# Expert gates of a PEER layer: one-hot matmuls against scattered, adding DMAs into a DRAM table

## What is computed

```python
sub = jnp.einsum("thpc,hpnc->thpn", qh, peer_sub_keys)
v1, i1 = lax.top_k(sub[:, :, 0], PEER_TOPK)
v2, i2 = lax.top_k(sub[:, :, 1], PEER_TOPK)
cand = (v1[..., :, None] + v2[..., None, :]).reshape(T, PEER_HEADS, 256)
vals, cidx = lax.top_k(cand, PEER_TOPK)
e1 = jnp.take_along_axis(i1, cidx // PEER_TOPK, axis=-1)
e2 = jnp.take_along_axis(i2, cidx % PEER_TOPK, axis=-1)
experts = e1 * N_KEYS + e2                      # 128 x 128
gates = jax.nn.softmax(vals, axis=-1)
...
h = jnp.einsum("cd,chkd->chk", xc, jnp.take(peer_u, experts))
a = jax.nn.gelu(h) * gates
y = jnp.einsum("chk,chkd->cd", a, jnp.take(peer_v, experts))
```

## Time and profile before

| | |
|---|---|
| median of 3 runs | 3204.29 us (3204.08 to 3206.46) |
| span of the profiled execution | 3203.0 us, mean granted clock 0.998 |
| its own time | the page gives the span alone; the three runs lie 1.1 to 3.5 us above it |
| busy: TensorE, weight loads, VectorE, ScalarE, GpSimd | 3185.0, 2707.6, 2226.0, 1555.5, 13.7 us |
| weight loads and other DMAs | 610.61 MB, 191 GB/s on the mean |

### The profile page before, as it was taken

The page is one execution under the profiler, slowest core; times in us unless marked ns, Lnnn a source line. Parts: engine busy times, 40 slices in busy tenths (PEclk is TensorE's granted clock), DMA queues, the critical chain, the costliest instruction groups (busy, mean ns, idle before and its releaser), DMA issues.

```text
span 3203.0 us, 42378 instructions
## 1 busy us (share of the span) xinstructions
PE 3185.0 (99%) x17362; PEld 2707.6 (85%) x17362; DVE 2226.0 (69%) x3055; ACT 1555.5 (49%) x1998; POOL 13.7 (0%) x29
## 2 busy tenths in 40 slices
PE   9999999999999999999999999999999999999999
PEld 8888888888888888887888888888888788888887
DVE  6775556677577567766568997766687787865564
ACT  4564444555355455546544555455443344444353
POOL 0000000000000000000000000000000000000000
PEclk9999999999999999999999999999999999999999
DMA  7456665656665666653555666666666665556665
GB/s 252 154 162 218 211 211 180 210 191 191 191 190 190 193 188 192 205 170 111 190 154 171 217 216 189 188 183 224 190 190 212 203 200 173 188 184 192 194 184 171
DMA packets 175825, 610.61 MB, mean 191 GB/s; under 512 B 19201, under 2 KB 27553, under 8 KB 174736
## 3 DMA queue, kind: packets, MB, share of 16 engines
q1 hardware_dynamic: 173648, 599.93, 60.0%
q0 software_dynamic: 1984, 7.99, 0.8%
HBM read 597.36 MB, written 10.49 MB: 190 GB/s over the span
## 4 chain that ended last, share of the span: by engine, by line
PE 97%; DVE 2%; ACT 1%; issue 0%; DMA 0%; SPq 0%; ACTq 0%; DVEq 0%
PE PS L1194 29%; PE PS L1211 16%; PE PS L1213 16%; PE PS L1212 16%; PE PS L1191 15%; PE PS L1414 1%; PE PS L1427 1%; PE PS L1293 1%; DVE LO L1749 0%; PE PS L1247 0%; PE PS L1326 0%; ACT UN L1506 0%; ACT HI L1436 0%; PE PS L1305 0%; PE PS L1223 0%
## 5 line engine op out<-in xcount | busy, mean ns | idle before, releaser
L1749 DVE TENSOR_TENSOR LO<-RAW,HI 128x1024 fp32r<-128x1024 f32 (+1 forms) x1096 | 1325.1, 1218 | 698.0 <-ACT HI L1436 694.7
L1436 ACT ACTIVATE HI<-RAW 128x1024 fp32r<-128x1024 f32 (+1 forms) x1096 | 1148.3, 1054 | 1044.6 <-PE PS L1213 732.5
L1194 PE MATMUL PS<-XX,HI 128*128 128x512 f32 x4032 | 968.4, 391 | 0.0
L1194 PEld LDWEIGHTS PS<-XX,HI 128*128 128x128 f32 x4032 | 739.4, 188 | 145.1 <-issue 2.4
L1211 PE MATMUL PS<-HI,FH 128*128 128x512 f32 x1760 | 692.0, 393 | 1.7 <-DVE LO L1749 1.7
L1213 PE MATMUL PS<-HI,FL 128*128 128x512 f32 x1760 | 685.8, 390 | 0.0
L1212 PE MATMUL PS<-LO,FH 128*128 128x512 f32 x1760 | 684.7, 389 | 0.0
L1191 PEld LDWEIGHTS PS<-XX,LO 128*128 128x128 f32 x4032 | 520.2, 191 | 21.1 <-issue 1.0
L1191 PE MATMUL PS<-XX,LO 128*128 128x256 f32 x4032 | 536.8, 284 | 0.0
L1213 PEld LDWEIGHTS PS<-HI,FL 128*128 128x128 f32 x1760 | 330.3, 188 | 70.1
L1211 PEld LDWEIGHTS PS<-HI,FH 128*128 128x128 f32 x1760 | 330.3, 188 | 69.1 <-DVE LO L1749 2.2
(11 more groups left out here) (286 smaller groups left out, 1667.7 us busy)
## 6 DMA issues: line engine op xcount, KB each, us to landing
RAW<-in_peer_ut SPq DMA_DIRECT2D x256, 512.0 KB, 4.1
RAW<-in_peer_v SPq DMA_DIRECT2D x256, 512.0 KB, 4.2
RAW<-in_ffn_w_up SPq DMA_DIRECT2D x176, 512.0 KB, 4.2
RAW<-in_w_in SPq DMA_DIRECT2D x88, 512.0 KB, 4.3
RAW<-in_ffn_w_down SPq DMA_DIRECT2D x88, 512.0 KB, 4.2
RAW<-in_w_in_c SPq DMA_DIRECT2D x48, 512.0 KB, 3.7
RAW<-in_w_mix_out SPq DMA_DIRECT2D x32, 512.0 KB, 4.0
RAW<-in_w_in_2c SPq DMA_DIRECT2D x32, 512.0 KB, 3.7
```

Of the source, the lines that this page charges most:

```text
L1194: m = e.matmul(o, hi[:, k, x], XX[:, 4 * u + k, :, :].rearrange("p h s -> p (h s)"), start=first and k == 0, stop=last and k == 3, skip_gr ...
L1436: return e.activation(dst, src, ACT.Copy) if scale is None else e.activation(dst, src, ACT.Copy, scale=scale)
L1749: return e.tensor_tensor(dst, src, hi.bitcast(F32), ALU.subtract)
```

## The change

The table of gates becomes a DRAM tensor of 16,384 x 256 floats (16 MB), with its row index second key first. SP fills it with zeros by 32 DRAM-to-DRAM copies of 512 KB beside the `f` products of the first block. Each `choose(t, g)` gets one more pause, then `address` (VectorE: table index = (second key x 128 + first key) x 256 + token) and `scatter` (GpSimd: 32 indirect DMAs of 128 single floats, each adding one column of gates at one column of indices; a head waits until the one before it has landed, since two heads can name the same expert for a token). When all have landed, GpSimd loads the gates of chunks 1 and 0, and later those of the other chunks, each in four pieces of 512 KB, into the same tiles `GM`. The steps `tables`, `onehot`, `gates_sum`, `gates_out`, `gates_aside`, `gates_back` and `gates_side` go, and with them rate 0.5. The waits of the weighing steps move to the pieces' semaphores. In the diff, `zero` is in SP's program, and `scatter` and `gates_in` are in GpSimd's.

```diff
+NKEY = 128
+ZEROS = 32
...
-                            ("sin", 128), ("invf", 8), ("iota", 128)])
+                            ("sin", 128), ("invf", 8), ("iota", 16), ("token", 2)])
...
+    put("token", np.arange(256).reshape(2, 128).T)
...
-    "gate": (0, 0, 3), "tables": (2, 0, 13),
-    "onehot": (0, 0, 3), "gates_sum": (1, 0, 0), "gates_out": (0, 3, 0), "gates_side": (1, 0, 2),
+    "gate": (0, 0, 3), "address": (0, 0, 2),
...
+    zeroed = [0]
     for n, th in enumerate(THIRDS):
         for q in th:
             for i in range(2):
                 for b in range(2):
                     product(("f", q, i, b), 4)
+                    if zeroed[0] < ZEROS:
+                        emit("zero", zeroed[0])
+                        zeroed[0] += 1
...
         emit("gate", t, g)
+        yield
+        emit("address", t, g)
+        emit("scatter", t, g)
...
-    def first_pass():
-
-        emit("onehot", 0, 0)
-        yield
-        for blk in range(32):
-            if blk < 31:
-                emit("onehot", 0, blk + 1)
-            yield
-            me = ("gates_sum", blk)
-            spare(me, 0, (ACT_, ("gates_out", blk), 3))
-            emit(*me)
-            emit("gates_out", blk)
-            if blk:
-                emit("gates_aside", blk - 1)
-        emit("gates_aside", 31)
-
-    def gates(r, pauses):
-        emit("onehot", r, 0)
-        yield
-        for blk in range(32):
-            if blk < 31:
-                emit("onehot", r, blk + 1)
-            yield from pause(pauses if blk % 4 else pauses - 1)
-            me = ("gates_side", r, blk)
-            spare_two(me, (DVE_, me, 2))
-            emit(*me)
-
-    def gates_back(c):
-        for n in range(4):
-            emit("gates_back", c, n)
-            yield
-            yield
-
-    def first_gates():
-        yield from pause(3)
-        me = ("tables",)
-        for t in range(2):
-            spare(me, t, (DVE_, me, 4 + 6 * t))
-        emit(*me)
-        rate[0] = 0.5
-        yield from first_pass()
-
+    def first_gates():
+        for c in (1, 0):
+            for j in range(4):
+                emit("gates_in", c, j)
+        yield
+
...
-    background.extend([gates_back(2), multiply_third()])
+    def gates_in(c):
+        for j in range(4):
+            emit("gates_in", c, j)
+
+    gates_in(2)
+    background.append(multiply_third())
     down(1, then=0)
-    background.append(gates(2, 3))
+    gates_in(4)
     down(0, then=2)
-    beside.append(gates_back(3))
+    gates_in(5)
     down(2, then=3)
+    gates_in(3)
     down(3, then=4)
-    background.extend([pause(4), gates(3, 3)])
+    gates_in(6)
     down(4)
+    gates_in(7)
...
+    IDX = at("IDX", [128, 2, NKEY], U32, offset=gb_at + 4 * K)
...
+    GATES_BY_PLACE = {0: (0, 3, 6), 1: (1, 2, 4, 7), 2: (5,)}
+
+    def gates_landed(c, j):
+
+        return l_gates[PLACE[c]][j], 16 * GATES_BY_PLACE[PLACE[c]].index(c) + 16
+
+    GATES = a["gates"].rearrange("(p x) o -> p (x o)", p=128)
...
-            elif kind == "gates_aside":
-                blk, = k
-                w.wait_ge(s_act, A("gates_out", blk))
-                e.dma_start(a["gates"][:, :, blk], PASS[:, blk % 2]).then_inc(l_pass[blk % 2], 16)
-            elif kind == "gates_back":
-                c, n = k
-                w.wait_ge(s_dve, V("second_mul", 3) if c == 2 else V("split_up", 2, 3))
-                for i in range(2):
-                    w.wait_ge(l_pass[i], 256)
-                e.dma_start(GM[PLACE[c]].rearrange("p c s -> p (c s)")[:, 1024 * n:1024 * n + 1024],
-                            a["gates"][:, c - 2, 8 * n:8 * n + 8].rearrange("p b x -> p (b x)")).then_inc(l_gates, 16)
+            elif kind == "zero":
+                n, = k
+                e.dma_start(GATES[:, 1024 * n:1024 * n + 1024], a["zeros"]).then_inc(l_zero, 16)
...
+            elif kind == "scatter":
+                t, g = k
+                w.wait_ge(l_zero, 16 * ZEROS)
+                w.wait_ge(s_dve, V("address", t, g))
+                for h in (2 * g, 2 * g + 1):
+                    if h:
+                        w.wait_ge(l_scatter[t], 256 * h)
+                    for i in range(16 * h, 16 * h + 16):
+                        e.indirect_dma_start(a["gates"], bass.IndirectOffsetOnAxis(IDX[:, t, i:i + 1], 0),
+                                             TK[:, t, i:i + 1], None, compute_op=ALU.add).then_inc(l_scatter[t], 16)
+            elif kind == "gates_in":
+                c, j = k
+                if c < 2:
+                    for t in range(2):
+                        w.wait_ge(l_scatter[t], 256 * 8)
+                else:
+                    w.wait_ge(s_dve, {2: V("second_mul", 3), 3: V("split_up", 2, 3), 4: V("third_mul", 3),
+                                      5: V("split_up", 0, 3), 6: V("split_aside", 3, 3), 7: V("split_aside", 4, 3)}[c])
+                e.dma_start(GM[PLACE[c]][:, 4 * j:4 * j + 4, :].rearrange("p c s -> p (c s)"),
+                            GATES[:, 4096 * c + 1024 * j:4096 * c + 1024 * j + 1024]).then_inc(l_gates[PLACE[c]][j], 16)
...
+            elif kind == "address":
+                t, g = k
+                first, second = (TK[:, t, 128 * n + 32 * g:128 * n + 32 * g + 32] for n in (1, 2))
+                w.wait_ge(l_const, 16)
+                w.wait_ge(s_dve, V("gate", t, g))
+                e.scalar_tensor_tensor(out=first, in0=second, scalar=float(NKEY), in1=first, op0=ALU.mult,
+                                       op1=ALU.add).then_inc(s_dve, 1)
+                w.wait_ge(s_dve, V("address", t, g, k=1))
+                e.tensor_scalar(IDX[:, t, 32 * g:32 * g + 32], first, float(S), const("token")[:, t:t + 1], ALU.mult,
+                                ALU.add).then_inc(s_dve, 1)
             elif kind == "first_mul":
                 j, = k
                 w.wait_ge(s_act, A("us_gelu", 0, j))
-                w.wait_ge(s_act, A("gates_out", 31))
+                w.wait_ge(*gates_landed(0, j))
                 d = blocks(GM[2], j)
                 e.tensor_tensor(d, d, blocks(GM[0], j), ALU.mult).then_inc(s_dve, 1)
             elif kind == "second_mul":
                 j, = k
-                w.wait_ge(s_pe, P("tables"))
                 w.wait_ge(s_act, A("us_gelu", 1, j))
-                w.wait_ge(s_act, A("gates_out", 31))
+                w.wait_ge(*gates_landed(1, j))
                 if j:
                     w.wait_ge(s_dve, V("second_mul", j - 1))
                 e.tensor_tensor(HB[:], blocks(STAGE, j), blocks(GM[1], j), ALU.mult).then_inc(s_dve, 1)
...
             elif kind == "third_mul":
                 j, = k
                 w.wait_ge(s_act, A("first_mul", j))
-                w.wait_ge(l_gates, 64)
-                d = by_eight(blocks(GM[0], j))
-                e.tensor_tensor(d, d, from_pass(2, j), ALU.mult).then_inc(s_dve, 1)
+                w.wait_ge(*gates_landed(2, j))
+                d = blocks(GM[0], j)
+                e.tensor_tensor(d, d, blocks(GM[1], j), ALU.mult).then_inc(s_dve, 1)
             elif kind == "split_aside":
                 c, j = k
                 w.wait_ge(l_back[j], 16 * (c - 2))
-                if c == 3:
-                    w.wait_ge(l_gates, 128)
-                    gates, hb, h = from_pass(3, j), by_eight(HB[:]), by_eight(blocks(UF, j))
-                else:
-                    w.wait_ge(s_dve, V("gates_side", 2, 31))
-                    gates, hb, h = blocks(GM[PLACE[4]], j), HB[:], blocks(UF, j)
+                w.wait_ge(*gates_landed(c, j))
                 w.wait_ge(s_dve, V("split_aside", c, j - 1) if j else V("split_aside", 3, 3) if c == 4 else
                           V("second_mul", 3))
-                e.tensor_tensor(hb, h, gates, ALU.mult).then_inc(s_dve, 1)
+                e.tensor_tensor(HB[:], blocks(UF, j), blocks(GM[PLACE[c]], j), ALU.mult).then_inc(s_dve, 1)
                 w.wait_ge(s_act, A(*step))
...
-                w.wait_ge(s_dve, V("gates_side", c // 2, 31))
+                w.wait_ge(*gates_landed(c, j))
...
+        "zeros": np.zeros((128, 1024), np.float32),
...
-    a["gates"] = nc.dram_tensor("gates", (128, 2, 32, 128), F32, kind="Internal").ap()
+    a["gates"] = nc.dram_tensor("gates", (NKEY * NKEY * S, 1), F32, kind="Internal").ap()
```

More of the change, by code:

```diff
@@ L63, in constants @@
     put("invf", np.tile(invf, (128, 1)))
-    put("iota", np.tile(np.arange(128), (128, 1)))
+    put("iota", np.tile(np.arange(16), (128, 1)))
+    put("token", np.arange(256).reshape(2, 128).T)
     return c
@@ L886, in _program @@
     HB = over("HB", [128, 4, S], 32 * K)
[L887 to L895, removed]
+    IDX = at("IDX", [128, 2, NKEY], U32, offset=gb_at + 4 * K)
     BP = at("BP", [128, 2, S], offset=const_at + 4 * CONSTS["mask2"][0])
-    TAB = at("TAB", [128, 2, S], BF16, offset=mask1_at)
-    KEYS2 = at("KEYS2", [128, 128, 2], BF16, offset=mask1_at + K)
     PS = ctx.enter_context(nc.psum_tensor("PS", [128, 4096], F32))
@@ L960, in _program @@
```

(58 more changed lines are left out.)

43 lines of the change are left out of this document (removed).

## The result

The changed kernel takes **3291.8 us**, median of 4 runs (3291.41 to 3293.64), beside 3204.5 (4 runs) of the kernel before on the same chip: ratio 1.0274 [1.026, 1.0289]. The forecast was 3148 with a range to 3270; the time moved the other way. Rival 1 came, at 3291.8 where it was priced at 3282.

A forecast was written before the change was run, and what follows sets the result against it. TensorE, 99% busy, was taken to bound the kernel; removing 25.9 + 27.5 + 0.6 + 1.7 = 55.7 us, with the additions costing nothing, took 3204.3 to 3148.6, forecast as 3148 us; own range 3138 to 3160, 8 in 10 reaching to 3270.

The forecast's parts named there:

- Rival 1: At VectorE's `first_mul`: the scatter ends late, at 2.0 us an indirect DMA, 134 us behind, giving 3282 us; chance 0.17.
- The base and the removal: TensorE paces the kernel; removing the small matmuls, the transposes and 1.7 us of idle time gains 55.7 us.
- the 5.56 us of two units: On TensorE: a pair of weight units without a gate step takes 5.56 us, with one 6.37.
- zeroing at nothing: The 32 zero copies on SP's queue beside the `f` products cost nothing; upper bound 166 us.
- `address` inside VectorE's free time: During `choose`: two small VectorE instructions for each of 8 (t, g), 3 us in all, fit VectorE's free time.
- VectorE at `first_mul`: The first multiplication, needing the gates, is due at 2116 us; VectorE may stand there 8 us more, until 2124.
- the loads: GpSimd's loads of the gates after the scatter: 12 us allowed to the fifth of the first eight.
- The landing waits: In GpSimd's scatter: one wait of about 4 us for landing in each of 8 (t, g).
- the price of an adding indirect DMA: In GpSimd's scatter: 1.1 us each, twice the direct DMA's 0.54; the scatter ends at 2014, loads by 2026, 90 us early.
- the threshold (1.48): Price in us of one indirect DMA at which scatter and loads end at 2124 and the gates are late.
- Rival 2: In `choose`: each indirect DMA holds VectorE for half its 1.1 us, 141 us against 28 free, giving 3261; chance 0.12.
- Rivals 3 to 5: Gain eaten, 3204, chance 0.04; zero copies delay loads, 3231, chance 0.05; removed small matmuls ran in gaps, 3200, chance 0.02.

The follow-up runs named there:

- `e1_half`: The changed kernel without the scatter of the second 128 tokens (128 of 256 indirect DMAs), whose gates stay zero; 3145.9 us, ratio to before 0.9818.
- `e4_zero_twice`: The changed kernel with each zero copy issued once more, into a second table that nobody reads; 3293.3 us, ratio to before 1.0274.
- `e7_hybrid`: The kernel before, with one-hot matmuls kept for chunks 0 to 3 and only chunks 4 to 7 reading the table; 3174.0 us, ratio 0.9907.

## Why the prediction was wrong

**What held.** The base and the removal: 55.7 us forecast, 59.9 measured in `e1_half`; the 5.56 us of two units; zeroing at nothing; `address` inside VectorE's free time; the start of the scatter (1702 forecast, 1700.5); VectorE at `first_mul` (2116 forecast, 2113.4), with 8 us of divided units in hand; the loads (12 forecast; 2260.45 - 2249.3 = 11.2). The landing waits were put at 32 us and took 22.9. Two slips in its sums change nothing: 3148.6 - 9 is 3139.6 and not 3138, and rivals 1 and 2 have 0.29 together (0.40 is all five).

**The step that failed** is the price of an adding indirect DMA: "I take twice the lower, 1.1 us, nearest to the direct row". It is 2.05 us, in three pieces, of which the estimate had one, and that too small. Put into the forecast's own formula (start 1702, 8 groups, 4 us of landing each, 12 of loads, due with cover 2124):
- the row alone, 1.54: 1702 + 8(32 x 1.54 + 4) + 12 = 2140, 16 us late; the time would have been 3164, still faster;
- with the gap of 0.30, 77 us more: 93 late, 3241;
- with the 0.22 that VectorE's two-operand instructions hold it, 56 more: 149 late, 3297. Measured are 3291.8.

So the row was under by 0.44, and two costs that no direct DMA has decided it. The direct rows follow each other without a gap and aren't held; they were evidence for a direct DMA alone. The forecast named the threshold (1.48) and the whole way down to the idle TensorE behind VectorE, and gave it 0.17, on the ground that nearly three times the direct row was wanted. Between 0.54 and 4.1 us, with a threshold at 1.48 inside, nothing in the trace spoke for the lower side; adding and reading indices are each work that the direct DMA doesn't do.

**Rival 2** had the right pair and the wrong side. It let the indirect DMA hold VectorE, and priced 141 us there. It is GpSimd that waits: VectorE has 82.66 us busy in `choose`, `divide` is as long as before. As GpSimd had become the bound, its 56 us count in full; I had taken "GpSimd, always working" as free of that. **Rivals 3 to 5** did not come: the zero copies delayed nothing (`e4_zero_twice`), and the matmuls removed were in line.

**What stays open.** Why an indirect DMA leaves 0.30 us behind it: the gap is there with and without adding, with VectorE at work and idle. And 4 us of the 59.9: the removed work gave more than its rows sum to. `e7_hybrid`, which leaves out the second and third pass alone, gained 30.1 for the 27.5 + 1.7 of its rows, so most of the 4 belongs to the first pass, or to the clock before it (1.00 in 1600 to 1660 us of the profiled `e1_half`, 0.97 in that of the kernel before). Not tried: leaving part of the first pass to the table as well; its steps are 25.9 us, so that by estimate such a kernel could come down from 3174 towards 3148.

## What to carry to other kernels

An engine that is idle has a throughput, and work moved to it has a due time: before taking the work of 96 matmul steps off TensorE, work out how many of the new operations fit before their first reader, and put every part of their cost (row, gap, hold, landing) against that. Where the price isn't in the trace and the threshold lies between the bounds, the chance belongs on both sides; and a trial of the operation by itself settles it. If the new producer is late, look for readers that come later before giving up the change: here the later half of the readers kept half of the gain with the same producer.

## What the runs showed of the hardware

- GpSimd, DMA of 128 words of 4 bytes between SBUF and DRAM: direct 0.54 us; with a list of 128 indices 0.955; with adding in DRAM besides 1.54. Behind each indirect one 0.30 us, behind direct ones none.
- An indirect DMA that GpSimd starts while VectorE runs an instruction with two SBUF operands is held for about what that one has left to run (0.94 us where 1.06 were left; 54.3 of 55.8 us fall on the 93 of 256 that start in a `divide`). VectorE isn't slowed (1215 ns for 1213), direct DMAs aren't held (550 ns at most), and those that start in a TENSOR_TENSOR with one operand in PSUM (22, 0.06 us in sum) or in one of VectorE's searches (0.11 us at most) are hardly longer.
- 64 copies of 512 KB from DRAM to DRAM within 432 us, 266 GB/s together with the weight loads (193 in the kernel before), cost TensorE nothing: it is busy in all of the 432 us.
- After 143 us of idle TensorE started at the lower clock level (granted 0.50), and its first 8 matmuls took 3.78 us, not 1.83.
